# Weight splits behind the root of four normalisations, and the forgetting attention's output layer cut into three parts

## The reference

```python
def modulate(x, g, shift, scale):
    return rmsnorm(x, g) * (1.0 + scale) + shift
# for each layer i:
hn = modulate(h, norm_g[i, 0], shift, scale)
m = s5_mixer(...) if i == 0 else fox_mixer(...)   # fox ends in: return o @ w_out
h = h + gate * m
hn = modulate(h, norm_g[i, 1], shift, scale)
f = conv_ffn(hn, ...)
h = h + gate * f
# second block: h = rmsnorm_2(h, norm_in_g) of the first block's normalised output
```

## Time and profile before

| | us |
|---|---|
| median of 3 runs (lowest to highest) | 1805.43 (1804.14 to 1806.81) |
| the profiled execution's own time | 1802.59 |
| its span, first to last instruction | 1800.9 |
| PE busy (share of the span) | 1682.4 (93%) |
| DVE busy | 1073.3 (60%) |
| ACT busy | 713.7 (40%) |
| DMA, mean | 110 GB/s |
| granted TensorE clock, mean | 0.971 of 2.4 GHz |

### The profile page before, as it was taken

One profiled execution on the slowest core, in us unless ns is written; L12 is line 12 of the kernel. 1 busy time (PEld: TensorE's weight loads), 2 busy tenths in 40 slices (PEclk: granted clock), 3 DMA queues, 4 the chain that ended last, 5 costly groups with the idle time before them and its releaser, 6 DMA issues.

```text
span 1800.9 us, 25420 instructions
## 1 busy us (share of the span) xinstructions
PE 1682.4 (93%) x9800; PEld 1336.3 (74%) x9800; DVE 1073.3 (60%) x1665; ACT 713.7 (40%) x1075; POOL 88.9 (5%) x130
## 2 busy tenths in 40 slices
PE   4979989999999989999879999999989999888997
PEld 2868768888888767777568888888777777765786
DVE  8899876665566655656455553455655564646443
ACT  4432433332333344444433332233436664545331
POOL 0063200000000000000000000000000000000000
PEclk9979999999999989999989999999989999999998
DMA  8342752434433535433022223321321221211231
GB/s 341 104 100 73 249 195 88 154 125 158 163 140 114 166 107 178 131 126 120 24 94 70 93 80 106 106 104 59 106 91 49 71 70 50 74 53 51 63 122 47
DMA packets 48533, 198.79 MB, mean 110 GB/s; under 512 B 8080, under 2 KB 13040, under 8 KB 34880
## 3 DMA queue, kind: packets, MB, share of 16 engines
q1 hardware_dynamic: 35776, 154.52, 24.9%
q0 software_dynamic: 12672, 43.10, 7.2%
HBM read 192.71 MB, written 4.23 MB: 109 GB/s over the span
## 4 chain that ended last, share of the span: by engine, by line
PE 79%; DVE 6%; issue 6%; ACT 5%; DMA 1%; POOL 1%; SPq 1%; DVEq 0%; ACTq 0%; POOLq 0%
PE ps L499 24%; PE ps L501 23%; PE ps L500 23%; ACT w_hi L935 3%; PE ps L590 2%; PE ps L603 2%; PE ps L615 2%; DVE w_lo L1386 2%; DMA ada<-in_ada_k 1%; PE ps L758 1%; ACT pw L1038 1%; POOL Mtz L318 1%; PE ps L734 1%; ACT sq L1029 0%; PE ps L674 0%
## 5 line engine op out<-in xcount | busy, mean ns | idle before, releaser
L499 PE MATMUL ps<-xn_hi,w_lo 128*128 128x512 f32 x1264 | 510.4, 404 | 22.3 <-DVE xn_lo L1521 9.6
L501 PE MATMUL ps<-xn_hi,w_hi 128*128 128x512 f32 x1264 | 498.7, 395 | 0.0
L500 PE MATMUL ps<-xn_lo,w_hi 128*128 128x512 f32 x1264 | 498.0, 394 | 0.0
L1386 DVE TENSOR_TENSOR w_lo<-raw,w_hi 128x2048 fp32r<-128x2048 f32 (+1 forms) x145 | 311.9, 2151 | 233.5 <-ACT w_hi L935 233.2
L935 ACT ACTIVATE w_hi<-raw 128x2048 fp32r<-128x2048 f32 (+1 forms) x145 | 260.1, 1794 | 147.4 <-PE ps L501 138.2
L499 PEld LDWEIGHTS ps<-xn_hi,w_lo 128*128 128x128 f32 x1264 | 241.3, 191 | 82.0 <-issue 22.1
L501 PEld LDWEIGHTS ps<-xn_hi,w_hi 128*128 128x128 f32 x1264 | 240.7, 190 | 51.9
L500 PEld LDWEIGHTS ps<-xn_lo,w_hi 128*128 128x128 f32 x1264 | 241.8, 191 | 46.9
L499 PE MATMUL ps<-act_hi,w_lo 128*128 128x512 f32 x352 | 139.7, 397 | 2.4 <-DVE w_lo L1386 2.4
L501 PE MATMUL ps<-act_hi,w_hi 128*128 128x512 f32 x352 | 139.2, 396 | 0.0
L500 PE MATMUL ps<-act_lo,w_hi 128*128 128x512 f32 x352 | 139.2, 395 | 0.0
(11 more groups left out here) (383 smaller groups left out, 2415.3 us busy)
## 6 DMA issues: line engine op xcount, KB each, us to landing
raw<-in_weights SPq DMA_DIRECT2D x97, 1024.0 KB, 4.9
adaw<-in_ada_w POOLq DMA_DIRECT2D x64, 512.0 KB, 4.7
raw<-in_weights SPq DMA_DIRECT2D x16, 768.0 KB, 4.2
raw<-in_weights SPq DMA_DIRECT2D x16, 640.0 KB, 3.8
ada<-in_ada_k SPq DMA_DIRECT2D x8, 1024.0 KB, 17.8
rot<-in_ada_w POOLq DMA_DIRECT2D x16, 512.0 KB, 4.9
fbias<-f_dram SPq DMA_DIRECT2D x16, 256.0 KB, 4.0
raw<-in_weights SPq DMA_DIRECT2D x8, 512.0 KB, 3.5
```

Of the source, the lines that this page charges most:

```text
L499: pe.matmul(bank, lo_w, hi_x, start=start, stop=False)
L500: pe.matmul(bank, hi_w, lo_x, start=False, stop=False)
L501: return pe.matmul(bank, hi_w, hi_x, start=False, stop=stop)
L1386: V.tensor_tensor(w_lo[:, b, 0:words], raw[:, b, 0:words], f32(w_hi[:, b, 0:words]), ALU.subtract).then_inc(split_lo, 1)
```

## The change

1. Norms ffn0, mix1, ffn1 and in2: the second chunk's split moves on ACT behind the root, on DVE behind the reciprocal (for in2 behind its whole root chain) and ahead of the wait for the spread and of the tiles. A small product (`gain`) in in2 moves ahead of that wait too.
2. fox_out (4 chunks of 8 k-tiles) becomes fox_oa (columns 512 to 1023, k-tiles 0 to 5, 2 chunks of 1536 words), fox_ob (columns 0 to 511, all k-tiles, 2 chunks of 2048) and fox_oc (columns 512 to 1023, k-tiles 6 and 7, 2 chunks of 512). Columns 512 to 1023 are thus added to `h` twice. PE runs fox_oa and fox_ob up to k-tile 6 between the beats, three beats to five steps, then k-tile 7 of fox_ob, then fox_oc.
3. DVE adds fox_oa's chunks to `h` and splits fox_ob's in periods 27 and 29 (ACT splits there too). The split of the first up10 chunk moves on DVE behind the last residual, on ACT behind the third; fox_oc's splits come right behind fox_ob's residuals, ahead of their squares' sums. `modulation(3)` moves ahead of the residuals.
4. In s5_out's last chunk all three `ada` stand ahead of the residual (before: one ahead, two behind).

```diff
-        LAYERS += [("fox_out", 8, 256, 4)]
+        LAYERS += [("fox_oa", 6, 256, 2), ("fox_ob", 8, 256, 2), ("fox_oc", 2, 256, 2)]
...
PE
-                between = spread(beats, (0,), 1)
-                first = FIRST["fox_out"]
+                between = spread(beats, (0, 1, 3), 5)
+                layer("fox_oa", fo_hi, fo_lo, (o_done, 0), between=between)
+                first = FIRST["fox_ob"]
                 for n in (first, first + 1):
-                    product("fox_out", n // 2, n % 2, fo_hi, fo_lo, (o_done, 0), between, (0, 6))
-                for n in (first, first + 1):
-                    product("fox_out", n // 2, n % 2, fo_hi, fo_lo, (o_done, 0), between, (6, 7))
+                    product("fox_ob", n // 2, n % 2, fo_hi, fo_lo, (o_done, 0), between, (0, 7))
                 for _ in beats:
                     pass
                 for n in (first, first + 1):
-                    product("fox_out", n // 2, n % 2, fo_hi, fo_lo, (o_done, 0), None, (7, 8))
-                for n in (first + 2, first + 3):
-                    product("fox_out", n // 2, n % 2, fo_hi, fo_lo)
+                    product("fox_ob", n // 2, n % 2, fo_hi, fo_lo, (o_done, 0), None, (7, 8))
+                layer("fox_oc", lambda k: fo_hi[:, 6 + k], lambda k: fo_lo[:, 6 + k])
...
ACT
+            if behind_root:
+                behind_root()
             rounded(name, dst_hi, shift)
...
+                        if p in (3, 5) and g == 3:
+                            split_next(FIRST["fox_oa"] + p // 2)
...
                 for i in range(4):
-                    n = FIRST["fox_out"] + i
-                    split_next(n + 1)
+                    n = FIRST["fox_ob"] + i
+                    if i < 2:
+                        split_next(n + 1)
                     residual("ffn1")(n // 2, n % 2, i)
-            if l == 0:
-                split_next(FIRST["up00"])
-            norm(f"ffn{l}", xn_hi, shift=2 * l + 1)
+                    if i == 2:
+                        split_next(n + 1)
+            norm(f"ffn{l}", xn_hi, shift=2 * l + 1, behind_root=lambda: split_next(FIRST[f"up{l}0"]))
...
DVE
             norm_stat(name)
+            if behind_root:
+                behind_root()
             norm_spread(name)
...
+                        elif p in (3, 5):
+                            n = FIRST["fox_oa"] + p // 2 - 1
+                            residual(2, None)(n // 2, n % 2, 2 + p // 2 - 1)
+                            split_next(n + 1)
...
+                modulation(3)
                 for i in range(4):
-                    n = FIRST["fox_out"] + i
-                    residual(2, "ffn1")(n // 2, n % 2, i)
-                    split_next(n + 1)
-                modulation(3)
+                    n = FIRST["fox_ob"] + i
+                    residual(2, "ffn1", then=(lambda: split_next(n + 1)) if i < 2 else None)(n // 2, n % 2, i)
+                split_next(FIRST["fox_oc"] + 1)
...
ACT and DVE, the last pair of down of each layer's second half
-                        split(j + 1, b)
+                        if not (last and b):
+                            split(j + 1, b)
```

More of the change, by code:

```diff
@@ L432, in _ @@
             upto(after)
-            following = ("fox_q2", "fox_q3", "fox_out")[g]
+            following = ("fox_q2", "fox_q3", "fox_oa")[g]
             upto(following, 1)
             load_bias(2 * g + 2)
-            following, count = (("fox_k2", 1), ("fox_k3", 1), ("fox_out", 2))[g]
+            following, count = (("fox_k2", 1), ("fox_k3", 1), ("fox_oa", 2))[g]
             upto(following, count)
@@ L983, in residual, with norm @@
             return evacuate
-        def norm(name, dst_hi=None, width=D, shift=None):
+        def norm(name, dst_hi=None, width=D, shift=None, behind_root=None):
             i = NIDX[name]
@@ L1202, in _ @@
             if l:
-                norm("mix1", xn_hi, shift=2)
+                norm("mix1", xn_hi, shift=2, behind_root=lambda: split_next(FIRST["fox_q0"]))
                 act.wait_ge(in_fw, 16)
@@ L1226, in _ @@
                         if p == 0 and g == 3:
-                            split_next(FIRST["fox_out"])
+                            split_next(FIRST["fox_oa"])
+                        if p in (3, 5) and g == 3:
+                            split_next(FIRST["fox_oa"] + p // 2)
                         if g < 3:
@@ L1266, in _, with down @@
                 squares = (f"mix1" if l == 0 else "in2") if hf == 1 else None
-                def down(i):
+                def down(i, last=False):
                     for b in range(2):
@@ L1271, in down @@
                         residual(squares, 1)(j, b, i * 2 + b)
-                        split(j + 1, b)
+                        if not (last and b):
+                            split(j + 1, b)
                 with act.Fori(0, DT // 2 - 1) as i:
                     down(i)
-                down(DT // 2 - 1)
-        norm("in2", xn_hi)
+                down(DT // 2 - 1, last=hf == 1)
+        norm("in2", xn_hi, behind_root=lambda: split_next(FIRST["sb_q0"]))
         layer("sb_q0", copy_out(b_q, HD ** -0.5), early=True)
@@ L1459, in add_square, with residual @@
             V.tensor_tensor(ssq[:], ssq[:], sq[:, r], ALU.add).then_inc(ssq_ready, 1)
-        def residual(gate, squares, tiles=2, permuted=False):
+        def residual(gate, squares, tiles=2, permuted=False, then=None):
             def evacuate(j, b, i):
@@ L1474, in evacuate @@
                     ins.then_inc(evac[b], 2 // tiles)
+                if then:
+                    then()
                 if squares:
@@ L1533, in norm_tiles, with norm, ada_norm @@
                 low(n - 1)
-        def norm(name, *args, **kwargs):
+        def norm(name, *args, behind_root=None, **kwargs):
             norm_stat(name)
+            if behind_root:
+                behind_root()
             norm_spread(name)
             norm_tiles(name, *args, **kwargs)
-        def ada_norm(name, a):
-            norm(name, lambda m: h[:, m], lambda m: gain[:, a, m:m + 1], lambda m: mod[:, a, m:m + 1], xn_hi, xn_lo)
+        def ada_norm(name, a, following):
+            norm(name, lambda m: h[:, m], lambda m: gain[:, a, m:m + 1], lambda m: mod[:, a, m:m + 1], xn_hi, xn_lo,
+                 behind_root=lambda: split_next(FIRST[following]))
         def gated(name, src, dst_hi, dst_lo):
@@ L1854, in out_and_ada @@
         def out_and_ada(j, b, i):
-            ada(28 + 3 * i, 1)
+            ada(28 + 3 * i, 3 if i == 3 else 1)
             into_h(j, b, i)
-            ada(29 + 3 * i, 2)
+            if i < 3:
+                ada(29 + 3 * i, 2)
         layer("s5_out", out_and_ada)
@@ L1865, in _ @@
                 modulation(2)
-                ada_norm("mix1", 2)
+                ada_norm("mix1", 2, "fox_q0")
                 dve.wait_ge(fw_hi, 1)
@@ L1891, in _ @@
                         elif p == 0:
-                            split_next(FIRST["fox_out"])
+                            split_next(FIRST["fox_oa"])
+                        elif p in (3, 5):
+                            n = FIRST["fox_oa"] + p // 2 - 1
+                            residual(2, None)(n // 2, n % 2, 2 + p // 2 - 1)
+                            split_next(n + 1)
                 for n in (32, 33):
                     fox_period(n)
+                modulation(3)
                 for i in range(4):
-                    n = FIRST["fox_out"] + i
-                    residual(2, "ffn1")(n // 2, n % 2, i)
-                    split_next(n + 1)
-                modulation(3)
-            if l == 0:
-                split_next(FIRST["up00"])
-            ada_norm(f"ffn{l}", 2 * l + 1)
+                    n = FIRST["fox_ob"] + i
+                    residual(2, "ffn1", then=(lambda: split_next(n + 1)) if i < 2 else None)(n // 2, n % 2, i)
+                split_next(FIRST["fox_oc"] + 1)
+            ada_norm(f"ffn{l}", 2 * l + 1, f"up{l}0")
             tiles = sum(HALVES) * l
@@ L1950, in _ @@
                             ada_loop(i * 2 + 70, b)
-                down(DT // 2 - 1)
+                down(DT // 2 - 1, last=hf == 1)
         norm_stat("in2")
+        split_next(FIRST["sb_q0"])
+        TT(gain[:, 0], par[:, PCOL["final_g"]:PCOL["final_g"] + DT], par[:, PCOL["norm_in_g"]:PCOL["norm_in_g"] + DT], ALU.mult).then_inc(rc2, 1)
         norm_spread("in2")
-        TT(gain[:, 0], par[:, PCOL["final_g"]:PCOL["final_g"] + DT], par[:, PCOL["norm_in_g"]:PCOL["norm_in_g"] + DT], ALU.mult).then_inc(rc2, 1)
         dve.wait_ge(rc2, 3)
@@ L2106 @@
             w[f"{name}{g}"] = fox[:, n * D + 256 * g:n * D + 256 * (g + 1)]
-    w["fox_out"] = a["fox_w_out"][0]
+    fox_o = a["fox_w_out"][0]
+    w["fox_oa"], w["fox_ob"], w["fox_oc"] = fox_o[:6 * P, 512:], fox_o[:, :512], fox_o[6 * P:, 512:]
     F = FT * P
```

## The result

| | before | changed |
|---|---|---|
| median (lowest to highest, runs) | 1804.79 (1803.66 to 1806.81, 4) | 1793.74 (1793.06 to 1794.82, 4) |
| the profiled execution's own time | 1802.59 | 1793.06 |
| its span | 1800.9 | 1791.4 |
| PE busy | 1682.4 (93%) | 1675.8 (94%) |
| granted clock, mean | 0.971 | 0.975 |

The ratio is 0.9938 (0.9921 to 0.9955). Forecast were 1798.9 and a range of 1794.5 to 1806.5: the direction is right, the time lies 0.8 us under the range. A second measurement of both kernels gave 0.9952 (0.9938 to 0.9966, experiment 5). The medians thus put the gain at 11 and at 9 us, above the 6.5 forecast, though the second interval, 6 to 11 us, just takes 6.5 in.

The account below looks back on a forecast made before the run. PE, 79% of the span, bounds the kernel through waits and low-clock stretches. Fox -5.9 us (+14.4 up to k-tile 7, -20.3 behind) and other norms -0.65 give -6.5: 1805.43 becomes 1798.9, range 1794.5 to 1806.5.

Parts of the forecast that it names:

- the 5.18 us wait: After the attention, PE's wait for fox_out's third chunk's split; forecast to go, within -20.3 us from k-tile 7 to ffn1's tiles.
- Period 25's wait: PE's wait for ACT's copy in the attention, forecast to go from 3.9 to about 1.6 us: -2.3.
- the clock behind it: After period 25's wait the clock was 0.57 over 4 us; forecast to stay up: -1.7 us.
- the cover of the 1.42 us: PE's wait for the last output tile after the attention, forecast covered by six steps of fox_ob, 4.2 us: -1.4.
- the sum up to K: The attention up to the start of k-tile 7 (K): 24 more steps less saved waits, forecast +14.4 us, K = 910.6.
- +4.0: New PE waits at the second transpositions of periods 28 and 30, behind the 2048-word splits: 2.0 us, twice.
- a few tenths: Slack forecast for PE's second transposition, which waits for the first copy, in periods 28 and 30.
- Rival 1: The two splits stand in series with the attention, 5.6 instead of 2.0 us each: +7.2, 1806.1; chance 0.17.
- rival 2: Waits at second transpositions of periods 28 and 30 exceed 3.9 us, the clock falls: +14.5, 1813.4; chance 0.10.
- Rival 3: The waits of periods 28 and 30 vanish, ACT's copy ending sooner: -4.0, 1794.9; chance 0.13.
- rival 4: Norms do nothing or lose, fox wins alone; longer PE wait before first tile keeps clock low: 1801.5; chance 0.15.
- a sign of being wrong: If the norms lose, the split between root and tile is dearer than 4.2 us.

Follow-up runs that it names:

- experiment 5: The changed kernel once more, unedited: 1795.41, ratio 0.9952.
- experiment 1: The changed kernel with the four norms' splits and the order of `ada` as before, leaving only the output layer's division: 1791.86, ratio 0.9933.
- experiment 6: The changed kernel with the norm ffn1 alone as before, its second split ahead of the root: 1791.29, ratio 0.9932.
- experiment 3: The kernel before once more, unedited: 1804.01 (one run).
- experiment 9: The changed kernel, DVE's splits of fox_oa's second and fox_ob's chunks inside the following period, all four norms' second-chunk splits among the tiles, `ada` as before: 1784.68, ratio 0.9889.
- experiment 10: The changed kernel with DVE's seven sums of squares for ffn1 cut from 512 columns to 1: 1792.78, ratio 0.9934.

## Why the prediction was right in kind and short in size

**Right.** That the change wins at the output layer and by what: the 5.18 us wait gone, the slow stretch behind it gone, the layer's tail cut to DVE's chain. Period 25's wait (1.56 against 1.6), the clock behind it and the cover of the 1.42 us came as forecast. Once the two waits are set at their measured size, the sum up to K is 13.0 against 12.6 measured. The first tile came 19.9 and 20.7 us behind K (20.9 forecast). mix1 gave -0.4 (-0.5), in2 -0.25 (-0.15), ffn0 0 to +0.3 (0).

**The step that failed** is the term "+4.0" for "two waits of 2.0" at the second transpositions of periods 28 and 30: they took 1.57 + 1.07 = 2.64. DVE did start 3.14 us behind period 28's scores, where I had 3.1, and the first copy ended 5.55 behind them, where I had 3.1 + 2.4 = 5.5. What I mis-sized is PE's slack, "a few tenths", of which I used 0.1. Three steps now stand ahead of the second transposition where the old order had two, so PE came to it 4.12 us behind the scores (878.09 - 1.57 - 872.40). An undelayed chain would have let it go at 1.04 + 2.41 + 0.14 = 3.59: a slack of 0.5, and 2.1 - 0.5 is the 1.57. Period 30 has two key tiles where 28 has four: its exponentials and division are shorter, the copy ends 1.92 us behind DVE's start instead of 2.41, and that is the other 0.5 (DVE starts 0.2 later there, 3.35 us behind the scores, and PE comes 0.2 later, 4.35 behind them, which cancels). I had taken one price for two periods of different width.

**Smaller terms, all to the same side.** A chain of DVE instructions is shorter than the sum of their durations, since the next starts 0.05 to 0.1 us before the listed end. The earlier trace rows had shown it (900.74 + 1.49 = 902.23, and the next starts at 902.14), and over the instructions from K to the last add it makes 11.2 into 10.5 us. Second, fox_oa's first chunk is smaller by a quarter, and its splits in period 23 take 1.48 and 1.76 us instead of 1.90 and 2.29. I had left that out. The stage ahead of the output layer (mix1's first matmul to the output layer's) is shorter by about 0.5 us: on average 199.9 in the four traces with the old layer and 199.5 in the eight with the divided one. Single traces scatter by as much, and that the split is the cause is argued, not shown.

**By the stages**: -8.7 (the second pair -7.8) for output layer and ffn1's norm, -0.5 for the stage ahead, -0.65 to -0.35 for the other norms, so -8.7 to -9.9 against -6.5. Of the difference 1.4 is the two waits, 0.4 the rest up to K, 0.2 to 1.0 the tail, 0.5 the stage ahead. These terms together take the forecast from 1798.9 to between 1795.6 and 1796.4, which the range still held. The last 1.9 to 2.7 us down to 1793.74 no stage accounts for. The medians stood 11.05 us under before at first and 8.7 in the second measurement, and executions of one kernel spread over 2 to 7 us; I take the rest to be this scatter, which no run shows.

**The rivals.** Rival 1, the splits in series, and rival 2, the lost clock, did not happen: three waits of 1.1 to 1.6 us within 32 us left the granted clock at 1.00. The Trainium skill (TensorE: Matmul & The Clock Gate, HAM oscillation) has a PE that waits between short bursts throttled each time, but tells it of longer waits, for DMA; the rows of 861 to 895 show these shorter ones without it, and so neither bear it out nor speak against it. Rival 3 went a third of the way. Of rival 4, that the norms do nothing or lose and fox wins alone, the outcome came true for the divided kernel, by the stages (experiments 1 and 6), for another reason than the one I gave. The cause is the split between root and tiles, which I had named as a sign of being wrong: in ffn1 of the divided layer it costs 1.5 to 2.3 us, more than the other three norms give back. The longer stretch at the lower clock, my reason, does not show: ffn1's first matmul to in2's last add takes 365.5 us in experiment 1 and 365.8 and 366.2 in the changed kernel, and 364.9 to 366.2 over all traces. I priced ffn1's tail as a whole, split behind the root included, and never against the split ahead of it; there the sums of 2.8 to 3.6 us and the spread would have covered it, while in mix1 L557 is done beforehand and leaves little to hide behind.

On the table load, the root started 1.29 us behind the load's start again (640.28 to 641.57). The Trainium skill (ScalarE: Activation LUTs, What ACT_TABLE_LOAD costs) adds a drain of 1.38 us to it; as forecast, no trace here shows that.

## What to carry to other kernels

When a step moves into a new order, take the waiting engine's slack from the new order, and each occurrence at its own size; the slack of 0.1 us taken here for both periods was 0.5 in one and more in the other. A split (or any work for the next layer) belongs where another engine's sums run anyway, or among the first tiles of the next layer, and hardly ever alone between root and tile: there it won 0.25 to 0.4 us in two norms of the changed kernel and cost 1.5 to 2.3 in a third. Before filling a wait, ask what the clock behind it costs: here 2.3 us behind a wait of 5.2.

## What the runs showed of the hardware

The forecast took it that a PE wait of 2.9 us keeps the clock. The same wait, in the second block, did so in some executions and not in others. Timeline row and 4 us stretches of the changed kernel, first (kept):

```profile
1656.05 0.41 PE L603 MATMUL ps<-ident,pw 128*128 128x128 f32 x2 [2.90 <-ACT sq L1029]
```
```profile
1654.00:1658.00 4.00, 1.95 (x6) 0.95 (x7) 2.02 (x8) 1.98 (x6) 0.00 (x0) 1.00 0.77 266
1658.00:1662.00 4.00, 3.33 (x23) 2.15 (x21) 3.42 (x10) 2.10 (x6) 0.00 (x0) 1.00 0.00 0
```

and of the same kernel in experiment 5 (lost):

```profile
1658.09 0.66 PE L603 MATMUL ps<-ident,pw 128*128 128x128 f32 x2 [2.88 <-ACT sq L1029]
```
```profile
1654.00:1658.00 4.00, 1.20 (x7) 0.63 (x5) 3.74 (x10) 1.60 (x5) 0.00 (x0) 0.90 0.47 143
1658.00:1662.00 4.00, 3.92 (x7) 1.70 (x8) 0.32 (x1) 0.38 (x1) 0.00 (x0) 0.50 0.30 125
```

The kernel before did the same (2.91 kept, 2.90 lost in experiment 3). All twelve traces have this wait, with 2.88 to 2.91 us. Eight kept the clock, and from the end of the wait to the end of the span they take 135.3 to 135.4 us. Four lost it (experiments 3, 5, 9 and 10) and take 137.0 to 137.1. The lost clock is thus worth 1.7 us, a part of the scatter between executions of one kernel; from in2's first matmul to the end they differ by more (483.7 to 484.5 us against 486.2 to 488.6), and the rest lies ahead of the wait. So a wait of 2.9 us does not settle what the clock does, as the forecast took it to, and no bound between 2.9 and 3.9 us can be read from the traces. The three waits of 1.1 to 1.6 us kept the clock in all five traces that have them (the changed kernel twice, experiments 1, 6 and 10).
